# Copying the upper half of a stick-breaking block's running sum behind its own addition

## What is computed

```python
z = einsum('bhqd,bhkd->bhqk', q_blk, k) * scale
strict = key_pos < q_pos
log_fail = where(strict, log_sigmoid(-z), 0.0)
after = cumsum(log_fail, axis=3, reverse=True) - log_fail
w = where(strict, exp(log_sigmoid(z) + after), 0.0)
return einsum('bhqk,bhkd->bhqd', w, v)
```

## Time and profile before

| | us |
|---|---|
| median of three runs | 3067.83 (3067.7 to 3069.32) |
| profiled execution | 3069.4 |
| its span, first to last instruction | 3067.7 |
| PE busy in the span | 2715.6 (89%) |
| DVE busy | 1480.9 (48%) |
| ACT busy | 1295.6 (42%) |
| POOL busy | 1039.0 (34%) |
| mean granted PE clock | 0.936 of full |

### The profile page before, as it was taken

One profiled execution on the slowest core, in us unless ns is written; L12 is line 12 of the kernel. 1 busy time (PEld: TensorE's weight loads), 2 busy tenths in 40 slices (PEclk: granted clock), 3 DMA queues, 4 the chain that ended last, 5 costly groups with the idle time before them and its releaser, 6 DMA issues. The chain is left out here.

```text
span 3067.7 us, 40579 instructions
## 1 busy us (share of the span) xinstructions
PE 2715.6 (89%) x13104; PEld 2222.6 (72%) x13104; DVE 1480.9 (48%) x2547; ACT 1295.6 (42%) x2794; POOL 1039.0 (34%) x713
## 2 busy tenths in 40 slices
PE   5689999878999998998668668888778999998999
PEld 4567777657788887887558667777667688887887
DVE  5646666744755553111562236666744755553111
ACT  4436656644333332222552246666634433332222
POOL 2025555540544443443101011111120544443443
PEclk8789999999999999999779779999989999999999
DMA  3111000041222223454111000000041222223454
GB/s 111 30 47 29 28 27 27 7 172 69 83 82 82 82 82 144 143 172 144 42 28 44 23 12 19 18 18 18 9 170 69 83 82 82 82 82 138 140 171 140
DMA packets 143097, 232.38 MB, mean 76 GB/s; under 512 B 17056, under 2 KB 93856, under 8 KB 143008
## 3 DMA queue, kind: packets, MB, share of 16 engines
q1 hardware_dynamic: 143008, 231.24, 22.7%
HBM read 182.98 MB, written 48.23 MB: 75 GB/s over the span
## 5 line engine op out<-in xcount | busy, mean ns | idle before, releaser
L1527 POOL TENSOR_TENSOR l0s_run_lo<-l0s_run,l0s_run_hi 128x512 fp32r<-128x512 f32 (+3 forms) x144 | 177.6, 1233 | 199.5 <-DVE l0s_run_hi L1690 199.5
L365 POOL TENSOR_TENSOR l1f_dn_lo<-l1f_dn_raw,l1f_dn_hi 128x1024 fp32r<-128x1024 f32 x44 | 106.1, 2412 | 139.3 <-ACT l1f_dn_hi L431 139.3
L365 POOL TENSOR_TENSOR l0f_dn_lo<-l0f_dn_raw,l0f_dn_hi 128x1024 fp32r<-128x1024 f32 x44 | 106.1, 2413 | 138.0 <-ACT l0f_dn_hi L431 138.0
L82 PE MATMUL banks<-l1f_dn_hi,l1f_a_hi 128*128 128x512 f32 x352 | 139.2, 395 | 10.0 <-issue 5.3
L82 PE MATMUL banks<-l0f_dn_hi,l0f_a_hi 128*128 128x512 f32 x352 | 138.6, 394 | 9.3 <-issue 5.3
L82 PE MATMUL banks<-l1f_T_hi,l1f_op_hi 128*128 128x512 f32 x352 | 140.1, 398 | 6.2 <-DVE l1f_T_lo L538 6.0
L82 PE MATMUL banks<-l0f_T_hi,l0f_op_hi 128*128 128x512 f32 x352 | 140.1, 398 | 5.9 <-DVE l0f_T_lo L538 5.6
L84 PE MATMUL banks<-l0f_T_hi,l0f_op_lo 128*128 128x512 f32 x352 | 139.2, 395 | 0.0
L84 PE MATMUL banks<-l1f_T_hi,l1f_op_lo 128*128 128x512 f32 x352 | 139.0, 395 | 0.0
L83 PE MATMUL banks<-l0f_T_lo,l0f_op_hi 128*128 128x512 f32 x352 | 138.8, 394 | 0.0
L83 PE MATMUL banks<-l1f_T_lo,l1f_op_hi 128*128 128x512 f32 x352 | 138.7, 394 | 0.0
(11 more groups left out here) (482 smaller groups left out, 8654.7 us busy)
## 6 DMA issues: line engine op xcount, KB each, us to landing
l0f_raw<-in_w_ffn_gu_dram SPq DMA_DIRECT2D x22, 1024.0 KB, 5.2
l0f_dn_raw<-in_w_ffn_down_dram SPq DMA_DIRECT2D x44, 512.0 KB, 4.0
l1f_raw<-in_w_ffn_gu_dram SPq DMA_DIRECT2D x22, 1024.0 KB, 5.2
l1f_dn_raw<-in_w_ffn_down_dram SPq DMA_DIRECT2D x44, 512.0 KB, 4.0
hidden_rows<-l0f_hid SPq DMA_DIRECT2D x22, 512.0 KB, 2.7
l0f_a_raw<-hidden_rows SPq DMA_DIRECT2D x44, 256.0 KB, 3.1
hidden_rows<-l1f_hid SPq DMA_DIRECT2D x22, 512.0 KB, 2.7
l1f_a_raw<-hidden_rows SPq DMA_DIRECT2D x44, 256.0 KB, 3.1
```

Of the source, the lines that this page charges most:

```text
L82: pe.matmul(out, l_hi, r_hi, start=first, stop=False, skip_group_check=True)
L365: pool.tensor_tensor(dn_lo[e][:], dn_raw[e][:], as_f32(dn_hi[e][:]), ALU.subtract).then_inc(dn_lo_done, 1)
L1527: pool.tensor_tensor(run_lo[t % NR][:, f:HALF], run[t % NR][:, f:HALF], as_f32(run_hi[t % NR][:, f:HALF]), ALU.subtract).then_inc(run_spli ...
```

## The change

In DVE's step t, the copy to `run_hi` is that of block t instead of block t-1, and it stands behind the addition (L1694) instead of in front of it. It waits for that addition (or, in the four blocks without one, for L1680), and for the sums of block t-4, which last read the buffer that it writes. Every block is still copied once; steps beyond the last block copy nothing.

```diff
-                b = t - 1
-                if exists(b, g, last):
-                    f, r = first_col[b % NB], run[b % NR]
-                    if b % NB in chained:
-                        dve.wait_ge(run_added, NC * g + n_chained[b % NB] - (NC if b < 0 else 0))
-                    else:
-                        dve.wait_ge(sp_done, NB * g + b + 1)
-                    wait(dve, sums_made, g, NB, b - NR + 3)
-                    dve.tensor_copy(run_hi[b % NR][:, f:HALF], r[:, f:HALF]).then_inc(run_hi_done, 1)
                 if t in chained:
                     fn, r = first_col[t - 2], run[t % NR]
                     dve.wait_ge(sp_done, NB * g + t + 1)
                     dve.tensor_tensor(r[:, fn:HALF], r[:, fn:HALF], run[(t - 2) % NR][:, fn:HALF],
                                       ALU.add).then_inc(run_added, 1)
+                if t < NB:
+                    f, r = first_col[t], run[t % NR]
+                    if t in chained:
+                        dve.wait_ge(run_added, NC * g + n_chained[t])
+                    else:
+                        dve.wait_ge(sp_done, NB * g + t + 1)
+                    wait(dve, sums_made, g, NB, t - NR + 3)
+                    dve.tensor_copy(run_hi[t % NR][:, f:HALF], r[:, f:HALF]).then_inc(run_hi_done, 1)
```

## The result

The changed kernel is slower: median 3076.61 us (3071.28 to 3076.88, 9 runs) against 3067.83 (3064.91 to 3073.91, 9 runs) for the kernel before on the same chip, ratio 1.0023 with an interval of 1.0013 to 1.0033. A second measurement on another chip gave 3073.84 (11 runs) against 3069.39 (35 runs), 1.0014 (1.0005 to 1.0022). The medians put the cost at 8.8 and 4.5 us; by the ends of the two intervals it is 1.5 to 10 us. The forecast was 3068.2 with a range of 3062 to 3074; the first median lies outside it, on the slow side, and the second, 3073.84, just inside.

The account below looks back on a forecast made before the run. PE was taken to bound the turns before the last, with 18 us of run_lo waits at stake. Terms +0.3 (first turn), -0.4 (ordinary turns) and +0.5 (last turn) gave +0.4 us: 3068.2 us, range 3062 to 3074.

Parts of the forecast that it names:

- What bounds the kernel: Upper-half copy stage: PE bounds the projecting turns; in the last DVE is busiest after it; run_lo waits total 18.0 us.
- Place two, the middle of the last turn: Blocks 8 to 15: POOL's subtraction holds DVE's addition, 2.36 us a block against 2.21; +1.25 at block 14's sums.
- The rival in which ACT's pace decides: Last turn: addition held little or not at all, blocks 7 to 15 at 2.04 us; 3065.0 us in all, chance 0.20.
- Looped turns, the queue: Start of four ordinary turns: l0s_q copy 0.15 us later, run_lo waits shrink; -0.1 a turn, -0.4 for four.
- the first turn's term: First turn's start: only 0.2 us of run_lo waits and the same l0s_q wait as in ordinary turns; +0.3 us.
- The slower rival: Turn starts: an added DVE neighbour costs 1.2 us in five turns, 6.0, plus 1.1 in last turn; 3075.3 us, chance 0.11.

Follow-up runs that it names:

- without the hold: Changed kernel with the addition L1685 replaced by an equally wide operation reading PSUM and one SBUF tile, running sum left out: ratio 1.0005 against the kernel before.
- with the weight subtractions out of the way: POOL's four weight subtractions moved from step 23 to steps 5 and 6 of the next turn: 0.9999 in the kernel before, 0.9992 in the changed kernel.
- the filler: Changed kernel with eight more matmuls a turn, adding nothing to the result, ahead of PE's l0s_q wait: 3070.8 against 3067.59 us for the kernel before, 1.0007.
- the looped part alone: Kernel before with the new order only in the four looped turns and the first turn's last block: 3070.00 against 3069.39 us, 1.0001.
- the three profiles shown first: Last turn in old order: kernel before 60.64 us, new order in looped turns alone 60.60, new order in first turn alone 63.50.
- the other two edits: Later POOL weight subtractions, and DVE's bank copies ahead of the splitting; each alone in the changed kernel: 0.9992 and 0.9999 against the kernel before.
- the combined kernel: New order except in the last turn's blocks 6 to 19, later weight subtractions, bank copies ahead of splitting: 3062.73 against 3069.59 us for the kernel before, 0.9981.

## Why the prediction was wrong

**What bounds the kernel** held. PE is the bound in the looped turns: all of its waits for run_lo there are gone, the wait for l0s_q has grown by more (2.55 us a turn against 1.4 + 0.65 before), and a turn is 0.04 us shorter. "Last turn (about 564 to 637 us)" was read too wide: by ACT's first operation it begins at 577.05, and in it DVE was already nearly as busy as PE. Nothing in the sum hangs on that, nor on the 25.03 us between the two turn starts, which are 225.03.

**Place two, the middle of the last turn**, held. The period was forecast at 2.36 and is 2.37; the subtraction at 1.28 is 1.28; the held addition, which the forecast has end 0.55 behind the subtraction, ends 0.54 behind it and takes 1.28. Timeline after, to be read against the earlier trace rows:

```profile
603.17 1.28 DVE L1685 TENSOR_TENSOR l0s_run<-l0s_run,l0s_run 128x512 f32<-128x512 f32 x1
604.49 0.43 DVE L1694 CAST l0s_run_hi<-l0s_run 128x512 fp32r<-128x512 f32 x1
605.00 1.29 POOL L1527 TENSOR_TENSOR l0s_run_lo<-l0s_run,l0s_run_hi 128x512 fp32r<-128x512 f32 x1 [1.09 <-DVE l0s_run_hi L1694]
```

The sums of block 14 come 1.37 us later within the turn (1.25 forecast) and the last ones 0.81 (0.7, of which I took 0.5). The rival in which ACT's pace decides needed the hold to be absent; without the hold the blocks took 1.97 us each, about ACT's pace of 2.03, and the last turn 55.97. So the mechanism exists, and the hold is what shut it out.

**Looped turns, the queue.** The forecast was an l0s_q copy 0.15 later and a turn 0.1 shorter. It is 0.28 later, and the turn 0.04 shorter where the clock is full. As forecast, PE's waits for run_lo went and that for l0s_q grew, though to 2.55 and not to 1.5 to 2.

**The step that failed first is the first turn's term:** +0.3 forecast, +2.2 measured. I took it over from the looped turns and never laid out the first turn's own queue. In the loop the copy of block 0 was moved too, and the l0s_q copy comes only 0.28 later. My reading is that POOL, freed of its last subtractions sooner, holds DVE less there; it fits that with the weight subtractions out of the way the difference is larger, +0.42 (11.55 to 11.97), but it wasn't tested further. In the first turn POOL was idle there before (its waits were 1.25 and 2.25 us), nothing was to be gained, and each added neighbour and dependency counts: +1.03 of queue, of which 0.7 reach the end of the turn. The slower rival had this mechanism ("if one of the two added neighbours costs a full round", 1.2) but put it into all five turns at once; it holds in the one turn that I had not laid out.

**The step that is missing altogether is the clock.** My sum priced PE's waits by their length alone and as if four short ones were the same as one long one. Behind the one wait of 2.4 to 2.6 us into which they gathered, the granted clock fell: in the first turn (1.47 us, by the filler), and in a looped turn in some executions (1.4 us each: one turn in the second measurement, two in the looped part alone, none in the first profile). From the earlier trace rows I could have seen that the waits move together, and the earlier trace rows has a stretch whose clock is not full (0.97); I gave it no term. The trace before shows what that is: a fall as PE's wait of 1.60 us in the last turn ends, and none behind the longer one of 2.48.

```profile
580.53 0.80 PE L1774 MATMUL banks<-l0s_run_hi,upper 128*128 128x512 f32 x1 [1.60 <-POOL l0s_run_lo L1527]
...
588.12 0.33 PE L1774 MATMUL banks<-l0s_run_hi,upper 128*128 128x128 f32 x1 [2.48 <-POOL l0s_run_lo L1527]
```

```profile
580.00:584.00 4.00, 3.47 (x9) 1.66 (x10) 3.96 (x6) 0.90 (x2) 4.00 (x5) 0.57 0.00 0
...
588.00:592.00 4.00, 3.54 (x20) 2.36 (x21) 3.89 (x11) 2.48 (x8) 1.26 (x3) 1.00 0.00 0
```

So the trace before had a fall to be seen, but no length of wait from which one comes.

The sum by what was measured is 2.2 + 0.8 - 0.2 = 2.8 us for the first profile, and one looped turn with a clock fall more makes 4.2, which is the size of the second comparison (4.5 us). The first comparison, 8.8 us between medians of nine runs, would need some four more falls or something outside the stage, where executions differ by more than that (9.5 us between the fourteen profiles); its ratio's interval begins at 1.0013, 4.0 us, and I don't explain more than that.

**Open.** Why the clock falls behind a 2.53 us wait in one execution and not behind a 2.55 us one in another isn't settled: the instructions are the same. How much of the last turn's 0.8 us is the hold and how much the clock isn't parted either: with the old order that turn alone ranges from 60.60 to 63.50 in the three profiles shown first. How often it falls in executions that weren't profiled was not measured either; that the falls make up the rest of the timed slowdown fits the ratios, but is argued and not shown. The old order in the first turn and the looped turns' new order, with the old one in the last, was not run without the other two edits, so what each of the three gives in the combined kernel isn't parted beyond the single runs above.

## What to carry to other kernels

Lay out the queue of every variant of a loop body for itself (first, looped, last): the same added instructions put the l0s_q copy 0.28 us back in the looped turns, where DVE was being held anyway, and 1.03 in the first turn, where it wasn't. When an edit moves small waits of TensorE into one place, count the new wait as one piece and add the price of a clock fall to the slow side. Where two engines take turns at SBUF, bringing one's operation forward can do no more than change which of them is held, as in the last turn here; in the looped turns it paid (0.66 us each) once POOL's weight subtractions had been moved out of the way.

## What the runs showed of the hardware

A wait of PE of 2.5 us between dense stretches was followed by 3.4 us of half clock in some turns and by none in others: 76.40 against 74.97 us for the same turn with the same wait. So was one of 1.75 us (76.07 against 74.67). A fall also stood behind waits of 1.60 us (last turn before) and 1.55 (a first turn of 70.47 us, against 69.06 before), and none behind one of 2.48 (last turn before), while the first turn of the kernel before waits 1.33 without a fall and the combined kernel's 1.2 us waits had none behind them. With all but 0.9 us of the first turn's 2.4 us wait filled with matmuls there was none either.

A DVE addition of 128x512 with both inputs in SBUF takes 1.28 us when it starts inside a POOL subtraction and 0.68 when it starts ahead of it; the subtraction takes 1.28 in the first case and 1.66 in the second. One of the two pays in each of these blocks, and the chain is shorter if POOL does: 2.21 us a block before, 2.37 after.
